# Who begins the stores of the turned h, the order of the loads, and the last layer norm

## The reference, cut to what matters

```
h = concat(meta (16 rows), x (2048 rows, 1024 columns))        # float32
u = h @ w_in;  for 4 groups of 256 columns, window w = 2, 4, 8, 16:
    pooled = mean of the last w rows of u                       # causal
    y = (pooled - u) @ w_group
h = layer_norm(ALPHA * h + (y * scale) @ w_out, ln_mix_g, ln_mix_b)
gate, up = split(h @ w_gu)                                      # 2 x 2816 columns
h = layer_norm(ALPHA * h + (silu(gate) * up) @ w_down, ln_ffn_g, ln_ffn_b)
return h[16:]
```

## Time and profile before

| | busy us | share of the span | instructions |
|---|---|---|---|
| PE | 1675.6 | 96% | 7400 |
| PEld | 1382.5 | 79% | 7400 |
| DVE | 985.0 | 56% | 1055 |
| ACT | 580.5 | 33% | 790 |
| POOL | 604.1 | 35% | 405 |
| all 16 DMA engines | 51.8% of their span | 304.45 MB | |

### The profile page before, as it was taken

The page is one execution under the profiler, slowest core; times in us unless marked ns, Lnnn a source line. Parts: engine busy times, 40 slices in busy tenths (PEclk is TensorE's granted clock), DMA queues, the critical chain, the costliest instruction groups (busy, mean ns, idle before and its releaser), DMA issues.

```text
span 1749.5 us, 18980 instructions
## 1 busy us (share of the span) xinstructions
PE 1675.6 (96%) x7400; PEld 1382.5 (79%) x7400; DVE 985.0 (56%) x1055; ACT 580.5 (33%) x790; POOL 604.1 (35%) x405
## 2 busy tenths in 40 slices
PE   7999996898999999999989999999998999999997
PEld 6888874687788888888868888888886888888786
DVE  6648585496674443445565544445553434559657
ACT  5232322233433333333443333333332332332220
POOL 0000023100534655565456666656532000242002
PEclk9999998899999999999999999999998999999999
DMA  8433635737134645556565644555547534454532
GB/s 327 183 119 142 241 110 177 249 143 283 49 133 150 222 142 196 187 187 197 165 210 154 197 148 134 169 173 151 190 140 267 181 125 163 178 210 168 196 129 107
DMA packets 183977, 305.66 MB, mean 175 GB/s; under 512 B 7376, under 2 KB 131408, under 8 KB 174160
## 3 DMA queue, kind: packets, MB, share of 16 engines
q1 hardware_dynamic: 183888, 304.45, 51.8%
HBM read 216.86 MB, written 87.56 MB: 174 GB/s over the span
## 4 chain that ended last, share of the span: by engine, by line
PE 81%; DMA 7%; DVE 6%; ACT 2%; POOL 2%; issue 1%; SPq 1%; ACTq 0%; POOLq 0%; DVEq 0%
PE acc L984 39%; PE acc L1013 16%; PE acc L830 8%; PE turn L984 6%; PE acc L846 6%; PE turn L1013 5%; DMA raw<-fold_dram 2%; DMA hf_dram<-st_mix 2%; DVE split L1309 1%; DMA dwr<-w_down 1%; DVE sums L1342 1%; DVE fa L1442 1%; DVE dw L1520 1%; PE turn L818 1%; DMA nat<-x_t 0%
## 5 line engine op out<-in xcount | busy, mean ns | idle before, releaser
L984 PE MATMUL acc<-fb,wf 128*128 128x512 f32 x1584 | 364.7, 390 | 8.0 <-DVE g L1574 6.6
L984 PE MATMUL acc<-fa,wf 128*128 128x512 f32 x1584 | 368.0, 392 | 3.5 <-DVE acc L1546 3.5
L984 PEld LDWEIGHTS acc<-fb,wf 128*128 128x128 f32 x1584 | 298.2, 188 | 70.7 <-issue 7.0
L984 PEld LDWEIGHTS acc<-fa,wf 128*128 128x128 f32 x1584 | 297.2, 188 | 65.6 <-issue 3.9
L1013 PE MATMUL acc<-dw,da 128*128 128x512 f32 x1386 | 319.1, 392 | 8.2 <-DVE da L1514 7.0
L1013 PEld LDWEIGHTS acc<-dw,da 128*128 128x128 f32 x1386 | 261.6, 189 | 64.6 <-DVE da L1514 7.5
L1449 DVE TENSOR_TENSOR wf<-wt,wf 128x512 fp32r<-128x512 f32 x132 | 128.7, 975 | 181.1 <-ACT wf L1142 180.9
L1449 DVE TENSOR_TENSOR wf<-wr,wf 128x512 fp32r<-128x512 f32 x176 | 174.2, 997 | 81.5 <-ACT wf L1142 81.1
L846 PE MATMUL acc<-split,act_sb 128*128 128x512 f32 x768 | 181.5, 397 | 6.4 <-DVE split L1309 6.4
L1142 ACT CAST wf<-wr 128x512 fp32r<-128x512 f32 x176 | 108.8, 618 | 229.8 <-PE acc L984 222.3
L683 POOL TENSOR_TENSOR wt<-wr,wt 128x512 f32<-128x512 f32 x88 | 126.3, 1435 | 159.5 <-DVE wf L1449 159.2
(11 more groups left out here) (104 smaller groups left out, 1636.7 us busy)
## 6 DMA issues: line engine op xcount, KB each, us to landing
wr<-w_gu SPq DMA_DIRECT2D x44, 1024.0 KB, 5.0
dar<-af_dram SPq DMA_DIRECT2D x56, 704.0 KB, 4.7
af_dram<-g SPq DMA_DIRECT2D x33, 512.0 KB, 3.8
raw<-w_in SPq DMA_DIRECT2D x16, 1024.0 KB, 5.4
raw<-fold_dram SPq DMA_DIRECT2D x16, 1024.0 KB, 5.9
fs<-hf_dram SPq DMA_DIRECT2D x14, 1024.0 KB, 7.9
dt_raw<-w_down SPq DMA_DIRECT2D x22, 512.0 KB, 5.9
wt_dram<-dt_t SPq DMA_DIRECT2D x22, 512.0 KB, 4.0
```

The source lines that it names most:

```text
L984: mm = nc.tensor.matmul(dst, wf[:, slot, a, k, :], fa[half][i][:, v, :, k, :], start=i < 2 and k == 0 and n3 == 0, stop=k == KC - 1 and n3 ...
```

## The change

1. `store_pair` leaves SP. ACT issues the store of st behind its own last copy of the pair; POOL issues the store of ss behind its last sum.
2. SP's order: in block 3 the last chunk c_mix(3, 3) is loaded ahead of forms 4, 5, 6 (it was behind 6 and 4), and form 6 last. `load_form(NP + 6)` goes from the end of SP's round for unit 22 to its beginning, ahead of `load_unit(24)` and `store_a(10)`. In the down product the last `store_a` and `store_s` go from ahead of step 1's loads to behind the load of step 2, and the residual rows from 2 on are spread anew.
3. Two of the forms are split later within their unit: form 6 of half 0 and form 5 of half 1 go behind the `c_seeded` write. DVE's first `c22_made` write waits for all seven forms.
4. Last rows: a row is scaled in the step that finished it, not one later, and for rows of z1 the statistics of the second half of columns are taken in t = 5.

```diff
@@ -305,12 +305,15 @@
         TURN0 = 5
-        NEW_FORM = {(0, 1): NP - 2, (0, 2): NP - 1, (HALF_UNITS - 4, 3): NP}
+        NEW_FORM = {(0, 1): NP - 2, (0, 3): NP - 1, (HALF_UNITS - 4, 3): NP}
         NEW_FORM.update({(HALF_UNITS - 1, place): NP + q for place, q in ((1, 1), (3, 2), (5, 3))})
-        NEW_FORM.update({(HALF_UNITS, place): NP + q for place, q in ((0, 4), (1, 5), (4, 6))})
+        NEW_FORM.update({(HALF_UNITS, place): NP + q for place, q in ((0, 4), (3, 5), (4, 6))})
         TF0, TF_STEPS = 3, 2 * JF
+
+        def pair_forms(pi):
+            return hf_dram[pi // TT].rearrange("f j p n -> j p f n")[pi % TT]
         def turned_in(n):
@@ -406,14 +409,6 @@
                     sp.wait_ge(turn_done, 4 * pi)
                 for a in range(2):
                     sp.dma_start(nat[:, a, :], h_rows[:, half * 2 * TT + a * TT + j, :]).then_inc(pair_landed, 16)
-
-            def store_pair(pi):
-                half, j = pi // TT, pi % TT
-                forms = hf_dram[half].rearrange("f j p n -> j p f n")[j]
-                sp.wait_ge(turn_taken, 4 * pi + 4)
-                sp.dma_start(forms[:, 0:3, :], st_of(pi)[:, 1:4].rearrange("p f k t -> p f (k t)")).then_inc(st_stored, 16)
-                sp.wait_ge(ss_made, 4 * pi + 4)
-                sp.dma_start(forms[:, 3:NP, :], ss_of(pi).rearrange("p f k t -> p f (k t)")).then_inc(ss_stored, 16)
             def load_form(q):
                 half, i = q // NP, q % NP
@@ -564,21 +559,16 @@
             store_h(1, 0)
             load_x(3, 0)
             load_chunk(c_mix(2, 1), 1, fold_dram[1])
-            store_pair(0)
             load_x(3, 1)
             load_chunk(c_mix(2, 2), 0, fold_dram[2])
             store_h(1, 1)
-            store_pair(1)
             load_x(3, 2)
             store_h(1, 2)
             load_chunk(c_mix(2, 3), 1, fold_dram[3])
-            store_pair(2)
             store_h(1, 3)
             load_z(2)
             load_x(3, 3)
             load_chunk(c_in(3, 0), 0, w_in[0])
-            store_pair(3)
-
             load_chunk(c_in(3, 1), 1, w_in[1])
             load_chunk(c_in(3, 2), 0, w_in[2])
             load_form(0)
@@ -594,15 +584,17 @@
             load_chunk(c_mix(3, 2), 0, fold_dram[2])
             store_h(2, 3)
             load_z(3)
+            load_chunk(c_mix(3, 3), 1, fold_dram[3])
+            load_form(4)
+            load_form(5)
             load_form(6)
-            load_form(4)
-            load_chunk(c_mix(3, 3), 1, fold_dram[3])
-            load_form(5)
             load_unit(0)
             load_unit(1)
             for n in range(UNITS):
                 half, jj = n // HALF_UNITS, n // 2
+                if n == HALF_UNITS:
+                    load_form(NP + 6)
                 if n + 2 < UNITS:
                     load_unit(n + 2)
                 if n % 2 == 0 and jj:
@@ -623,8 +615,6 @@
                         sp.dma_start(gb[:, q, :], v.partition_broadcast(P)).then_inc(gb_landed, 16)
                 if turned_in(n + 1)[1] == 0:
                     load_pair(turned_in(n + 1)[0])
-                if turned_in(n - 1)[1] == 2:
-                    store_pair(turned_in(n - 1)[0])
                 if n == TURN0 + 3 * TT:
                     load_form(NP)
                     load_form(NP + 1)
@@ -634,8 +624,6 @@
                     load_form(NP + 3)
                     load_form(NP + 4)
                     load_form(NP + 5)
-                if n == HALF_UNITS:
-                    load_form(NP + 6)
                 if half and n % 2 == 1:
                     load_sa(jj - JF)
                 if n == UP_LAST - 3:
@@ -650,16 +638,18 @@
             load_hz(1)
             for k in range(DSTEPS):
                 t, m = k // MT, k % MT
-                if k == 1:
-                    store_a(2 * JF - 1)
-                    store_s(JF - 1)
                 if k + 3 == 2 * MT:
                     sp.wait_ge(s_stored, 64 * JF)
                     sp.wait_ge(a_stored, 48 * JF)
                 if k + 3 < DSTEPS:
                     load_da(k + 3)
-                if k + 2 < MT:
+                if k == 2:
+                    store_a(2 * JF - 1)
+                    store_s(JF - 1)
+                if k < 2:
                     load_hz(k + 2)
+                elif 3 <= k < 7:
+                    load_hz(k + 1)
                 if t + 1 < NP:
                     for q in {1: (0, 1), 4: (2,), 6: (3,), 7: (4, 5)}.get(m, ()):
                         load_dw(t + 1, q)
@@ -710,6 +700,9 @@
                 sub(ss[:, 1], ss[:, 0], a11).then_inc(ss_made, 1)
                 pool.wait_ge(ss_made, 4 * pi + 3)
                 sub(ss[:, 3], a12, ss[:, 1]).then_inc(ss_made, 1)
+                pool.wait_ge(ss_made, 4 * pi + 4)
+                nc.gpsimd.dma_start(pair_forms(pi)[:, 3:NP, :], ss.rearrange("p f k t -> p f (k t)")
+                                    ).then_inc(ss_stored, 16)
             def unit_t123(n):
                 b21, b11, b12, b22 = (wr[:, n % 2, q] for q in range(4))
@@ -1046,6 +1039,10 @@
                 slot = k % 2 if pi < TT else 1
                 nc.scalar.copy(st_of(pi)[:, :, k, :], turn[:, slot, :].rearrange("p (b t) -> p b t", t=P)
                                ).then_inc(turn_taken, 1)
+                if k == KC - 1:
+                    act.wait_ge(turn_taken, part + 1)
+                    nc.scalar.dma_start(pair_forms(pi)[:, 0:3, :], st_of(pi)[:, 1:4].rearrange("p f k t -> p f (k t)")
+                                        ).then_inc(st_stored, 16)
             def stage_u(b, i):
                 act.wait_ge(chunk_done, c_in(b, i) + 1)
@@ -1561,6 +1558,8 @@
                 dve.wait_ge(prod_done, NP * n + 5)
                 if gate:
+                    if jj == 0:
+                        dve.wait_ge(fa_lo, NP)
                     if jj and jj - 1 < JF:
                         dve.wait_ge(a_stored, 32 * jj)
                     elif jj:
@@ -1620,10 +1619,14 @@
             ROWS0 = BLOCKS * ADDS
+            def half_stats(r, h, zz):
+                nc.vector.bn_stats(stats[:, r, h, :], zz[:, h, :]).then_inc(stats_done, 1)
+
             def row_stats(r, zz):
-                for h in range(2):
-                    nc.vector.bn_stats(stats[:, r, h, :], zz[:, h, :]).then_inc(stats_done, 1)
-                dve.wait_ge(stats_done, ROWS0 + 2 * r + 2)
+                half_stats(r, 0, zz)
+                if r < MT:
+                    half_stats(r, 1, zz)
+                dve.wait_ge(stats_done, ROWS0 + 2 * r + 2 if r < MT else ROWS0 + 3 * MT + (r - MT) + 1)
                 nc.vector.bn_aggr(mv[:, r, :], stats[:, r].rearrange("p a b -> p (a b)")).then_inc(aggr_done, 1)
                 dve.wait_ge(aggr_done, BLOCKS * TT + r + 1)
                 nc.vector.tensor_scalar(var_eps[:, r:r + 1], mv[:, r, 1:2], EPS, None, ALU.add).then_inc(var_ready, 1)
@@ -1655,10 +1658,11 @@
                     pt, pm = (k - 1) // MT, (k - 1) % MT
                     if pt in (4, 6):
                         finish_row(pt, pm)
-                        if pm:
-                            scale_row(pt, pm - 1)
-                    if pt == 5 and pm == 0:
-                        scale_row(4, MT - 1)
+                        scale_row(pt, pm)
+                    if pt == 5:
+
+                        dve.wait_ge(taken, taken_by(5, pm))
+                        half_stats(MT + pm, 1, z1[:, pm])
                 if t + 1 < NP:
                     if 1 <= m <= 5:
                         down_w_lo(JF * (t + 1) + m - 1)
@@ -1667,7 +1671,6 @@
                             down_w_lo(JF * (t + 1) + p)
             take(DSTEPS - 1)
             finish_row(6, MT - 1)
-            scale_row(6, MT - 2)
             scale_row(6, MT - 1)
```

## The result

The median of four runs is 1710.12 us (1709.22 to 1712.51), beside 1748.49 us for the kernel before in four runs on the same chip. The ratio is 0.9773, with a 95% interval of 0.9761 to 0.9785. That is 38.4 us saved, where the prediction's sum said 47.

The account below looks back on a forecast made before the run. PE was taken as the bound, busy 1675.6 of 1749.5 us, so only its 73.9 us idle and half-clock stretches counted. Savings 20 + 8 + 5 + 2 + 9.5 + 2.5 = 47 gave 1703 us, range 1688 to 1726.

Parts of the forecast that it names:

- The forecast case: The parts' savings add up to a time of 1703 us, own range 1695 to 1712; chance 0.55.
- Part 1: Block 2, stores of pairs 0 to 3: earlier stores shorten PE's three waits for turned h; 20 us saved, ends 5 and 31.7.
- Part 2a: Last chunk of block 3, loaded earlier: PE's wait and half clock behind it go; 8 us saved, ends 5 and 8.
- Part 3, unit 0: Seed write moved ahead of form 6's low half: of PE's 3.5 us wait about 0.2 is left; 5 us saved with clock.
- Part 2b and 3, unit 22: Form 6 of half 1 asked for 6.2 us sooner, its cast 2 us sooner; 2 us saved, ends 0 and 8.
- Part 2c: Start of the down product: weights asked for before SP waits for POOL; 9.5 us saved, ends 5 and 9.7.
- Part 4: Last rows: 2.9 us saved at the end, 0.4 lost on PE before t = 5; net 2.5, ends 1.5 and 2.9.
- The signs that it named: Copies' waits 8 or 10 us, unit 0's seed under 1, unit 22 4 to 6, end of span 7.3 behind PE.
- A: Block 2: all waits for the turned h vanish, issue and landing being short; 11 us more, 1692 us; chance 0.15.
- B: POOL's issue of a store is slow, 4 to 9 us; 1718 us at the slow end; chance 0.16.
- C: Block 2: stores begin earlier but land no earlier, as transfers fill the engines; gain nothing, 1722 us; chance 0.10.
- D: Slower: POOL's issue holds up the weights' sums too; zero gain at 13.5 us an issue, 1764 at 16; chance 0.04.

Follow-up runs that it names:

- e4: Kernel before, with only the stores of the turned h begun by ACT and POOL, all loads in the old order: 1728.76 us, ratio 0.9878.
- e1: Changed kernel with SP loading forms 6 and 4 ahead of block 3's last chunk again: 1710.75 us, ratio 0.9777 to the kernel before.
- e2: Changed kernel with form 6 of half 0 split at its old place, ahead of the seed: 1713.86 us, ratio 0.9794 to the kernel before.
- e3: Changed kernel with unit 0's weights loaded right behind block 3's last chunk, ahead of forms 4, 5, 6: 1702.7 us, ratio 0.9731 to the kernel before.
- e6: e3 with the store of activations ahead of form 6 and the weights in unit 22: 1700.26 us, ratio 0.9717 to the kernel before.
- e8: Changed kernel with the last two stores ahead of step 1's loads again in the down product: 1718.26 us, ratio 0.9822 to the kernel before.
- e10: Changed kernel with both statistics behind the last product and rows scaled one step later again: 1714.06 us, ratio 0.9795 to the kernel before.
- e5: e3 with a second tile for the sums of pairs 1 and 3 in block 2: 1703.35 us, ratio 0.9732 to the kernel before.
- e9: e6 plus two sum tiles and block 1's rows stored earlier: 1699.92 us, ratio 0.9712 to the kernel before.
- e11: e5 with block 1's rows stored before the load of x's next piece is asked for: 1702.22 us, ratio 0.9727 to the kernel before.

## Why the prediction was right, and which term was off

The forecast case held: 1710.1 us is inside its own range (1695 to 1712), and all parts but one gained, as said.

- **Part 1**, forecast 20, measured 21.9 (21.0 alone, e4). The three waits were put at 1, 2.5 and 6 us and came as 1.0, 4.6 and 2.4: the sum was near (9.5 and 8.0), the pieces were not, so part of this agreement is luck. Landings were taken as 8 us each and were 7.5 and 4.1, counted from the end of POOL's issue; sums as 6.5 to 7 us a pair and were 8.9, since most of them took the long 2.0 to 3.3 us. Issue taken 1.5 us, measured 0.77 to 0.96. The one stretch at half clock, behind the 4.6 us, cost 1.6 (3.26 us at 0.51), where 1.7 was said for the third wait.
- **Part 2a**, forecast 8, measured 8.1 at the start of unit 0.
- **Part 3, unit 0**, forecast +5, measured -2.9: this term was mis-sized, and it is nearly all of the miss (7.9 of 8.2 us). The step that failed is "Moved ahead, about 0.2 is left", together with "the weights of unit 0 come behind the same number of bytes as before". The second sentence was true and was the warning: PE came 8 us sooner, the weights did not. The first took the seed's start from DVE's queue before, where only the form lay in front of it, and did not ask when the weights behind that queue land once the unit starts sooner. e1 shows the hand-over, e2 that the later split still saves 3.0 to 3.5 us, e3 that the weights are the cause.
- **Part 2b and 3, unit 22**, forecast 2, measured 0.8. The place of the store of activations was named as the limit, and e6 shows it for 1.9 of the 6.3 us; the load of the form is next, and it holds its cast.
- **Part 2c**, forecast 9.5, measured 9.8, and 8.1 when undone (e8).
- **Part 4**, forecast 2.9 at the end and 0.4 on PE; measured 2.9 and at most 1.0 (e10: 0.7 of it in the wait before t = 5). Undone it costs 3.5 to 3.9 us in all, of which the trace puts 2.2 on part 4 and the rest on block 2 and what follows it (e10).

**The signs that it named.** The copies' waits (8.0 us, ended by POOL's sums), the missing waits before the last chunk and near 1340 us, and 2.9 us less between PE's end and the end of the span came as said. Two did not: the wait at the seed of unit 0, called to be under 1 us, was 5.7, and unit 22 kept 7.2 instead of 4 to 6. The first of these is the failed term above.

**The rivals.** A (all copies' waits vanish, 1692) did not come: 8.0 us are left, and e5 shows that even without POOL's chain they turn into another wait. B (POOL's issue slow) fell to the 0.77 to 0.96 us of eight issues. The issue at 261.26 us ran while DVE summed (259.72 to 262.02 us) and was the longest, 0.96. The Trainium skill, "SBUF — State Buffer", section "SBUF: two separate sides", led to an estimate of 2.5 us more per issue in that place; this trace does not show it beside such a sum, and for this case the measurement decides. The page's figures are for a DVE copy; no issue in block 2 ran beside one. C (stores begin earlier, land no earlier) is refuted by the landings, 3.9 to 7.5 us where the earlier trace rows has 8.1 to 10.4, and by e4. D (slower) needed an issue of 13.5 us (its sum should start at 50, not 49, which makes it 13.7 and changes nothing).

## What to carry to other kernels

A load that unblocks one stage moves the start of the next; before counting that gain, look at when the next stage's own loads land and how long the chain behind them is, for if their slack was no more than the gain, the wait only changes its name. When a store is late, look first at what its queue waits for ahead of it: here the engines that made the data began the stores themselves, at 0.4 to 1.0 us a store, and it saved 21. And order the loads of a crowded stretch by which one is wanted first, all of them together; moved one by one they hand the wait around.

## What the runs showed of the hardware

- A DMA issued by POOL took it 0.77 to 0.96 us (eight issues of the changed kernel), one by ACT 0.37 to 0.39; SP took 0.36 to 1.74 for its stores of the same tiles before. POOL's stores landed in 4.7 to 10.9 us from issue; SP's of the same sums landed in 6.3 to 12.0.
- With two tiles for the sums, POOL could have a second store on its way. In e5, e9 and e11 it sat idle 0.69, 3.85 and 3.16 us ahead of issuing pair 2's store, until its store for pair 1 had landed, though the program asks for no such wait. Why is not shown.
- The clock was granted at half (or, over a stretch, near it: 0.68 in e5 behind 3.93 us) behind every wait of PE of 3.1 us and more from block 2 on, and at full behind those of 1.7 us and less. Between these it went either way: full behind 2.37 us in the changed kernel, half behind 2.15 us in e2 and near half behind 2.12 in e10, all at the same place of the program. The changed kernel behind 4.60, 2.37 and 5.71 us of waiting (windows of PE, all engines: stretch, us, busy (x) of PE, PEld, DVE, ACT and POOL, granted clock, DMA share, GB/s):

```profile
279.24:281.30 2.06, 2.06 (x9) 2.06 (x10) 0.64 (x3) 1.90 (x4) 0.43 (x1) 0.50 0.53 203
293.34:296.74 3.40, 3.40 (x18) 2.85 (x19) 0.00 (x0) 1.02 (x2) 0.43 (x1) 1.00 1.07 361
434.42:441.22 6.80, 6.80 (x20) 5.39 (x21) 5.49 (x4) 3.12 (x5) 5.26 (x3) 0.63 0.01 2
```

So a wait of 4.6 us cost 1.6 us on top of its length, and one of 2.1 to 2.4 us either nothing or some 1.5. In all, the matmuls of the changed kernel took 7.5 us less than before.
